# The attention brings the merge's first operands, three stages share one region of SBUF, and the first heads' keys come in during the last projections

## What is computed

```python
h = rmsnorm_2(x, norm1_g[l]) * (1.0 + sc1) + sh1
proj = jnp.matmul(h, w_in[l])
(fq, fk, fv, flog, dq, dk, dv, iq, ik, iw, g_fox, g_dsa) = jnp.split(proj, split_at, axis=-1)
...
out_fox = forgetting_attention(fq, fk, fv, log_f).reshape(B, S, W_FOX)
...
out_dsa = dsa_attention(dq, dk, dv, iq, ik, iw).reshape(B, S, W_DSA)

merged = (jax.nn.sigmoid(g_fox + b_gate[l, :D]) * jnp.matmul(out_fox, w_proj_fox[l])
          + jax.nn.sigmoid(g_dsa + b_gate[l, D:]) * jnp.matmul(out_dsa, w_proj_dsa[l]))
x = x + gt1 * jnp.matmul(merged, w_out[l])
...
y = hierarchical_moe(h2.reshape(B * S, D), ...)
```

## Time and profile before

| | before |
|---|---|
| median of 3 runs | 3177.18 us (3176.4 to 3182.06) |
| the profiled execution | 3174.93 us, its span in the trace 3172.5 us |
| busy share of the span | PE 87%, DVE 69%, ACT 40%, POOL 25% |
| last projections end, attention's first matmul | 1879.8 us, 1902.3 us |
| last store of the projections issued | 1880.4 us |
| attention's last matmul, merge's first | 2238.4 us, 2262.3 us |
| merge's second tile begins on PE | 2290.7 us |

### The profile page before, as it was taken

The page is one execution under the profiler, slowest core; times in us unless marked ns, Lnnn a source line. Parts: engine busy times, 40 slices in busy tenths (PEclk is TensorE's granted clock), DMA queues, the critical chain, the costliest instruction groups (busy, mean ns, idle before and its releaser), DMA issues. The chain is left out here.

```text
span 3172.5 us, 35752 instructions
## 1 busy us (share of the span) xinstructions
PE 2775.1 (87%) x13124; PEld 2220.5 (70%) x13124; DVE 2195.8 (69%) x2950; ACT 1267.6 (40%) x2069; POOL 803.1 (25%) x398
## 2 busy tenths in 40 slices
PE   6999999979588869969979977979599679999998
PEld 3777776755366658758867856768488568888887
DVE  5599975526699944844635878963354369999997
ACT  3222221110166721123224205656322057777775
POOL 1432210000111100000210006445312025656564
PEclk9999999988698889979989988989799779999999
DMA  6233347633445361226533237221523369999996
GB/s 219 96 106 115 110 148 268 209 124 115 161 179 190 149 235 63 93 62 145 128 94 81 100 79 144 54 45 25 217 93 113 128 242 377 386 379 387 386 382 224
DMA packets 244489, 543.44 MB, mean 171 GB/s; under 512 B 31126, under 2 KB 154118, under 8 KB 228051
## 3 DMA queue, kind: packets, MB, share of 16 engines
q1 hardware_dynamic: 174178, 436.48, 39.1%
q0 software_dynamic: 33840, 59.49, 7.5%
q10 hardware_dynamic: 36288, 45.09, 4.0%
HBM read 450.74 MB, written 108.06 MB: 176 GB/s over the span
## 5 line engine op out<-in xcount | busy, mean ns | idle before, releaser
L2549 DVE TENSOR_TENSOR e_low<-e_raw,e_high 128x4096 fp32r<-128x4096 f32 x99 | 437.9, 4425 | 64.2 <-ACT e_high L2543 64.2
L2543 ACT ACTIVATE e_high<-e_raw 128x4096 fp32r<-128x4096 f32 x99 | 359.5, 3633 | 26.9 <-DVE e_g L2498 26.9
L135 PE MATMUL banks<-h_high,w 128*128 128x512 f32 (+1 forms) x1088 | 309.5, 368 | 9.0 <-POOL w L365 4.4
L135 PE MATMUL banks<-p_w_high,p_high 128*128 128x512 f32 (+1 forms) x640 | 249.8, 390 | 14.7 <-DVE p_w_low L1594 14.7
L135 PE MATMUL banks<-p_w_low,p_high 128*128 128x512 f32 (+1 forms) x640 | 245.6, 384 | 0.0
L135 PE MATMUL banks<-p_w_high,p_low 128*128 128x512 f32 (+1 forms) x640 | 245.5, 384 | 0.0
L135 PEld LDWEIGHTS banks<-h_high,w 128*128 128x128 f32 x1088 | 195.4, 190 | 49.0 <-POOL w L365 4.8
L135 PE MATMUL banks<-e_high,e_xhigh 128*128 128x512 f32 x528 | 211.1, 400 | 7.1 <-issue 5.5
L496 DVE SCALAR_TENSOR_TENSOR acc<-img,taps,acc 128x1024 f32<-128x1024 f32 x160 | 209.8, 1311 | 5.7
L135 PE MATMUL banks<-e_high,e_xlow 128*128 128x512 f32 x528 | 208.0, 394 | 0.0
L135 PE MATMUL banks<-e_low,e_xhigh 128*128 128x512 f32 x528 | 207.5, 393 | 0.0
(11 more groups left out here) (501 smaller groups left out, 6612.8 us busy)
## 6 DMA issues: line engine op xcount, KB each, us to landing
e_raw<-in_exp_w SPq DMA_DIRECT2D x99, 2048.0 KB, 11.3
s_sums<-cumT SPq DMA_DIRECT2D x32, 768.0 KB, 4.5
w_raw<-in_w_in SPq DMA_DIRECT2D x20, 1024.0 KB, 6.7
s_X<-xtok SPq DMA_DIRECT2D x19, 1024.0 KB, 7.7
p_raw<-in_w_in SPq DMA_DIRECT2D x18, 1024.0 KB, 6.5
xbcT<-res ACTq DMA_DIRECT2D x20, 640.0 KB, 2.9
xtok<-xt ACTq DMA_DIRECT2D x20, 640.0 KB, 4.1
w_raw<-in_ada_w SPq DMA_DIRECT2D x12, 1024.0 KB, 5.8
```

Of the source, the lines that this page charges most:

```text
L135: last = pe.matmul(out, a, b, start=start and n == 0, stop=stop and n == len(pairs) - 1)
L2543: act.activation(self.high[p % HIGHS][:], self.raw[p % RAWS][:], ACT.Copy).then_inc(*self.high_done.up())
L2549: dve.tensor_tensor(self.low[p % HIGHS][:], self.raw[p % RAWS][:], self.high[p % HIGHS][:].bitcast(F32), ALU.subtract).then_inc(*self.low_ ...
```

## The change

One region `m_w_low` of 64 KB a partition, allocated at the right end of SBUF before the second block's projections, serves in turn as the weights of `close_first`, as the two pairs of buffers of the last projections (`SecondProducts.w`), as the two key buffers of the forgetting attention (`fox_buffers`), and as the merge's raw weights and their low parts. The stages attention and merge stand in one outer stage, and the `recycle` between them is gone; the engines still wait at the attention's end for its semaphores.

- After chunk 8 of the projections (pair 0's last use) DVE fills the unused rows of key buffer 0 and POOL issues `load_fox(0)`, while PE works on chunk 9.
- The attention's start issues `fv` and `load_fox(1)` with no wait for head pair 0. SP also loads merge's first gate tile.
- After the last scores of head pair 2, and of head pair 3, POOL issues four of the merge's eight weight loads into the buffer that they leave. After the last pair that needs the mask `far`, SP loads the gate bias into its place, and tile 0 of both attentions' outputs.
- The merge begins with `bring_g(0)`, then splits weight block 0, then tile 0's outputs, then blocks 1 to 7. The wait of the second `bring_g` for the weights is gone.
- The routing's small tables move into the buffer `dt`.

```diff
-        load_fox(0)
         sp.wait_ge(*far_emptied)
         sp.dma_start(far[:, :, SEQ - P:SEQ], dram["far"].rearrange("m p n -> p m n")).then_inc(*masks_in.up())
-        for e in (sp, pool):
-            e.wait_ge(*fox_in[0].at(6))
         sp.dma_start(fv[:], pv[:, :, C_FV:C_FV + 512]).then_inc(*values_in[0].up())
-        load_fox(1), load_tile(0), load_tile(1)
+        ahead.load_fox(1), load_tile(0), load_tile(1)
...
+        ahead.load_gates()
...
+                if (i, m) == (len(chunks) - 1, 0):
+                    for e in (dve, pool):
+                        e.wait_ge(*summed.at(NT * i))
+                    ahead.empty_fox(0)
+                    ahead.load_fox(0)
                 if not dots:
                     chosen.fill(5)
...
             if kind == "fox" and j == 0:
-                fox_used[c] = scored.now()
+                pool.wait_ge(*scored.now())
                 if c + 2 < 4:
-                    load_fox(c + 2)
+                    ahead.load_fox(c + 2)
+                else:
+                    for n in range(4 * (c - 2), 4 * (c - 2) + 4):
+                        ahead.load(n)
...
+            if pairs[i] == ("dsa", TOPK // P - 1, 3):
+                sp.wait_ge(*max_done[i, 1])
+                ahead.load_bias()
+                ahead.load_outputs()
...
+    def fox_buffers(self, b):
+
+        half = self.low[:, KD * b:KD * b + KD, :].rearrange("p k n -> p (k n)")
+        return [half[:, 2 * SEQ * n:2 * SEQ * n + 2 * SEQ].rearrange("p (e n) -> p e n", e=2) for n in range(4)]
+
+    def load(self, j):
+
+        of = self.dram[("w_proj_fox_2", "w_proj_dsa_2", "w_out_2", "w_out_2")[j // 2]].rearrange("(k p) n -> p k n", p=P)
+        k = 2 * (j if j >= 4 else j % 2) - (8 if j >= 4 else 0)
+        self.core.pool.dma_start(self.raw[:, 2 * j:2 * j + 2, :], of[:, k:k + 2, :]).then_inc(*self.w_in[j].up())
...
-        bring_o(0)
-        for j in range(8):
-            load_weights(j)
+        bring_g(0)
         pool.dma_start(wr[:, :, 0:NG], weights("router_w_grp_2")).then_inc(*router_in.up())
         pool.dma_start(wr[:, :, NG:NG + NE], weights("router_w_exp_2")).then_inc(*router_in.up())
+        split_weights(0)
         split_o(0)
-        for n in range(KD):
+        for n in range(1, KD):
             split_weights(n)
-        bring_g(0)
-        sp.wait_ge(*w_in[3].at(1))
...
-STAGES = (project_first, state_space, attentions, late)
+STAGES = (project_first, state_space, second_block)
...
-                if stage in (project_first, attentions):
+                if stage is project_first:
                     core.recycle()
```

More of the change, by code:

```diff
@@ L1552, in project_second @@
+def project_second(core, dram, tables, second, chosen, ahead):
     pe, dve, act, pool, sp = core.pe, core.dve, core.act, core.pool, core.sp
@@ L1567, in project_second @@
         plain_of = [u for u in range(len(units)) if kind(u) in ("fv", "gate")]
-        ready = {half: raw_in[half].now() for half in range(2)}
         def done(ins):
@@ L1906, in look_ahead, with attentions @@
                 core.sp.dma_start(raw[b][:], dram["w_in_2"].rearrange("(k p) n -> p k n", p=P)[:, 4 * b:4 * b + 4, C_FQ:C_FQ + 512]).then_inc(*raw_in[b].up())
[L1908 to L1912 removed]
+                second.ready[b] = raw_in[b].now()
+        close_first(core, dram, tables, hh, hl, hl_raw, rows, raw, look_ahead, ahead)
+        project_second(core, dram, tables, second, chosen, ahead)
+def attentions(core, dram, tables, ahead):
     with Stage(core) as s:
@@ L1923, in attend @@
+def attend(core, dram, tables, chosen, ahead):
     pe, dve, act, pool, sp = core.pe, core.dve, core.act, core.pool, core.sp
@@ L1925, in attend @@
     with Stage(core) as s:
-        far = s.sb("a_far", [P, 2, SEQ])
-        fkk, fq = ([s.sb(f"a_{k}{b}", [2 * HD, 2, SEQ], R32) for b in range(2)] for k in ("fkk", "fq"))
-        fkl, fq1 = ([s.sb(f"a_{k}{b}", [2 * HD, 2, SEQ], R32) for b in range(2)] for k in ("fkl", "fqone"))
+        far = ahead.bias[:].rearrange("p (m n) -> p m n", m=2)
+        fkk, fq, fkl, fq1 = zip(ahead.fox_buffers(0), ahead.fox_buffers(1))
         dkk, dkl = (s.sb(f"a_{k}", [2 * HD, SEQ], R32) for k in ("dkk", "dkl"))
@@ L2816, in look_ahead @@
                 sp.dma_start(to[:], row(dram[name])).then_inc(*rows_in.up())
-        merge(core, dram, tables, look_ahead)
+        with Stage(core) as sm:
+            ahead = Ahead(core, sm, dram)
+            attentions(core, dram, tables, ahead)
+            merge(core, dram, tables, look_ahead, ahead)
         y, g = s.sb("e_y", [P, 2, D]), s.sb("e_g", [P, 2, DE])
```

215 lines of the change are left out of this document (119 added, 96 removed).

## The result

The changed kernel takes 3160.7 us in the median of 5 runs (3157.55 to 3164.29), for 3177.18 before: a ratio of 0.9948, 95% interval 0.9936 to 0.996. That is 16.5 us less, where 30 were forecast. The profiled execution's span is 3155.4 us, for 3172.5. The prediction had the sense and missed the size; the case that came true is the third, "a new wait takes part of it".

The account below looks back on a forecast made before the run. PE was taken to bound the merge, and DVE's fixed order of work the attention's start, so waiting removed there is kept. 11.3 - 0.5 + 19.0 = 29.8 us off 3174.9 gave 3145.1, forecast as a 3147 us median, range 3139 to 3160.

Parts of the forecast that it names:

- a new wait takes part of it: Rival: late mask or values, fills, POOL's bursts, ACT table or stage end leave savings of 8 to 26 us; chance 0.24.
- The mask: Attention's start: 128 KB load has 4 us to land and is in time; at most 12.7, leaving 3 us of the gain.
- The 6.0 us of DVE's fills: Attention's start: after the barrier DVE clears the mask, 1.80, makes three fills, 3.54, and the last fill, 0.65.
- The bursts on POOL: End of head pairs 2 and 3: four weight-load issues each; the first costs nothing, the second 0.5 us, between 0 and 3.
- SP's loads of bias and outputs: Attention, behind a store of the eighth sparse pair: 24 pairs lie between them and the merge, so they cost nothing.
- the rival for a slower kernel: Attention's stores get stuck behind the bursts; it decides from 36 us, 18 for each burst; chance 0.03.
- POOL's nine issues: Attention's start: loads of head pair 1, tiles and sparse keys, before ended ahead of the first division, start 16 us sooner, costing nothing.
- The merge's start: No barrier and earlier loads: PE begins at 2256.3, tile 1 comes 16.7 us earlier; 19 us saved in sum.
- the table load: Merge's start: ACT's 1.28 us table load before the sigmoid is not in the path; if it is, 1.3 more.
- POOL went first: Merge's start: POOL's second gate addition, having waited, precedes DVE's first half of the outputs; 19 us saved, 23.5 if DVE goes first.
- the third gap: Merge's start before: PE stood 10.69 us ahead of tile 1, whose outputs took 28.77 us behind 8 MB of weights.
- The clock's part: Merge, behind tile 1's start: without the idle there is no half-speed stretch of PE's clock, 1.8 to 2 us more saved.

Follow-up runs that it names:

- m1: Changed kernel with SP issuing the mask at once, ahead of all other loads, and POOL's head pair 1 loads waiting until it landed: 3150.2 us, ratio 0.9921.
- m2: Changed kernel with only POOL's head pair 1 loads waiting until the mask has landed; SP still issues it behind DVE's clearing: 3153.9 us, ratio 0.9927.
- m3: Changed kernel with only SP issuing the mask at once, without waiting for DVE's clearing; POOL's loads start beside it: 3154.0 us, ratio 0.9912.
- experiment 4: c1 with the eight weight loads issued one behind each of eight attention pairs, instead of four behind one pair, twice: 3139.2 us, ratio 0.989.
- s1: Changed kernel with four attention output tiles and store semaphores instead of two, so ACT waits for the stores of four pairs before: ratio 0.9944.
- experiment 2: Changed kernel with the mask loaded ahead of head pair 1's loads, in three variants: m1 0.9921, m2 0.9927, m3 0.9912.
- g1: Changed kernel with POOL's bias addition to tile 1's gates waiting for the last of the eight low halves of the first weights: ratio 0.9925.
- c1: Changed kernel with m1, s1 and a reordered merge start, POOL's gate additions held until four and eight low halves are made: 3140.65 us, ratio 0.9888.
- c2: c1 with the eight weight loads issued one behind each of eight attention pairs instead of in two bursts of four: 3139.2 us, ratio 0.989.
- b1: The kernel before, unchanged, profiled once more: last matmul of the projections at 1882.1 us, 2.7 us later than in the first profile.
- c3: c2 with POOL's addition of bias to tile 0's gates moved into the attention's tail: 3135.42 us, ratio 0.9865.
- u1: Changed kernel with the three fills and six loads of head pair 0 put back at the attention's start: ratio 0.9945.

## Why the prediction was wrong

By its own steps, as spans of the two profiled executions (3172.5 - 3155.4 = 17.1 saved, 29.8 forecast):

- **The mask: wrong, 7.8 us, the main miss.** "I take it as in time, since it is 128 KB on a queue of its own." It was on its own queue and landed 12.0 us after its issue all the same, next to the bound of 12.7 that I had named and set aside. In m1, m2 and m3, where the mask is in before the large loads move, the wait is gone. The 6.0 us of DVE's fills held, and so did the 1.0 by which the stage begins later (measured 1.06). Before, the mask was issued 1.9 us behind the first load of head pair 0 in the same way (1888.42 and 1886.53), and nobody saw it, since DVE needed it only when those keys were in. The change frees DVE from the keys and puts the like 3 MB of head pair 1 at the same place.
- **The bursts on POOL: undersized.** 0 and 0.5 us forecast, 0.72 and 0.68 measured. "So the first burst costs nothing" read six loads at head pair 1 as free; but before, these take 13.28 us with them and head pair 2 takes 13.28 without, while four weight loads make it 14.00. The two 13.28 don't show that the issues are free: at head pair 1 they put POOL's next division off by 3.6 us, and only the one after the head's end came no later (experiment 4). Why that one does come later with four loads at head pair 2 is not settled.
- **The stores: in the wrong case.** "SP's loads of bias and outputs [...] cost nothing", and stores behind loads appeared only in the rival for a slower kernel, priced from 18 us a burst. SP's loads made ACT wait 3.3 us, and the attention was 1.5 us longer for it; a term of that size was missing. Another 1.5 us stand at the waits behind the loads of head pairs 2 and 3, which no other trace has (s1 above), and 0.3 at smaller differences, the granted clock's above all: these 1.8 are the execution's.
- **Given back: 0.8 us, not forecast.** "POOL's nine issues [...] ended ahead of the first division" misread the rows: they are eleven, and that division stood right behind the last of them (experiment 2). With the change they are over early, and from first maximum to first division it is 4.0 us for 4.8.
- **The merge's start: right in sum, partly for other reasons.** 16.7 us forecast up to tile 1, 17.4 measured; with what lies behind it 19.0 forecast (16.7 and 1.8 to 2 are 18.5 to 18.7; the sum was rounded up) and 19.7 measured; PE's first matmul 17.7 us after the attention for 17.9. POOL did hold DVE up (g1). But the table load was not hidden (1.28 us at 2249.09, behind POOL's addition), so ACT and DVE came later than I had it, and POOL was at work for 1.1 us when DVE asked. That POOL went first needed no rule for two waiting engines, then: it was simply there 1.1 us earlier. My reason, that an engine that has waited goes next, failed in c1 and c2. Of what is saved, the barrier and the start of all loads are 5.3 us, tile 0's loads 6.8, the eight weight loads 5.2; the earlier trace rows made me ascribe the third gap to the 8 MB alone.
- **Executions: 2.2 us** that the changed kernel's profiled run lost ahead of the attention (b1).

-29.8 + 7.8 (mask) + 0.9 (bursts, over the 0.5) + 1.5 (SP's loads) + 1.8 (execution, in the attention) - 0.8 - 0.7 (merge) + 2.2 (execution, ahead of it) = -17.1. Mask, bursts and SP's loads come back in the other traces; 4.0 us of the gap between these two traces are the executions'. The medians miss the forecast by 13.7 us (3160.7 for 3147), and what they hold beyond the terms that come back, no trace of these says.

The clock's part, 1.8 to 2 us at the merge, wasn't tested alone. What lies behind tile 1 took 878 to 882 us in thirteen of the fourteen traces and 885 in b1, so 2 us can't be read from it, nor can the 2.3 above.

## What to carry to other kernels

When a change takes a wait away, ask what else that wait had covered: here it had hidden a 128 KB load behind 3 MB, and the load was then what the first instruction stood for. Issue the small load that is needed first ahead of the large ones; a queue of its own didn't help here. Letting the large ones wait for it works too, but whatever stands behind their issues on the issuing engine comes later. Loads that are moved under other work need slack in that work's own small stores; four buffers instead of two gave it here. A DVE subtraction and a POOL addition that exclude each other are best scheduled where one of the engines has nothing to do, as in the attention's tail. And before a stretch that got longer is put down to an edit, read the granted clock there and the same stretch in other traces of the same code: here each was worth up to 1.5 us.

## What the runs showed of the hardware

- A 128 KB load issued 1.85 us behind the first of 3 MB on another queue landed after 12.0 us: no transfer of its own for 4.7 us, by when the other queue had made 316. Issued 0.44 us ahead of them (m3) it had begun all its transfers after 1.7 us, before the other queue's first. The Trainium skill (DMA: Bandwidth & Descriptors, Queues, rings and completion order) says that each DMA engine takes turns between the queues that have work, a packet at a time. The trace agrees once the mask's transfers run, 259 of one queue and 239 of the other in 3 us; it doesn't show what held the first of them for 4.7 us.
- POOL's addition, asked for during a series of seven DVE subtractions of two SBUF tiles, began only when the series ended (8.84 us for 4.5 in c1). In the changed kernel's merge POOL asked in the middle of such a series too, at 2281.43, and got in when the subtraction under way ended, though DVE had not paused either; DVE's next one then took 5.63 us for 1.22:

```profile
2280.13 2.35 DVE L2263 TENSOR_TENSOR m_w_low<-m_w_low_raw,m_wo_high 128x1024 fp32r<-128x1024 f32 x2
2281.43 5.51 POOL L2313 TENSOR_TENSOR m_gs<-m_gs,m_bg 128x2048 f32<-128x2048 f32 x1 [7.10 <-DMA m_gs<-proj]
2282.40 5.63 DVE L2263 TENSOR_TENSOR m_w_low<-m_w_low_raw,m_wo_high 128x1024 fp32r<-128x1024 f32 x1
```

  The Trainium skill (SBUF — State Buffer, SBUF: two separate sides) has whichever starts first hold the ports, and that section says nothing of the next. By these rows either can be next; what decides it was not tried.
- ACT's table load stood behind the wait of its instruction (2249.09, right after POOL's addition), and in the earlier trace rows ahead of one, as in c1, where it was done by 2241.3 and the sigmoid waited until 2247.31.
- PE's granted clock fell to half speed for 6.8 us in the large tiles of the attention in c2, g1 and m3, with 1.4 to 1.5 us more for the same divisions each time, and did not in c3, u1 or m1 at the same places.
